# Column-strip sums of squares ahead of three FFNs, and shorter settling groups, in a two-block transformer kernel

## The reference

```
def rms(x, g):   return x * rsqrt(mean(x*x, -1) + 1e-6) * g
def ffn(x):      h = rms(x, norm); return (silu(h @ w_gate) * (h @ w_up)) @ w_down   # 1024 -> 2816 -> 1024

for l in (0, 1):                                  # first block
    x = x + 0.5 * ffn1(x)
    h = rms(x, mix_norm);  q, k, v, ... , gates = split(h @ w_in)
    x = x + merged(three attention branches, gates) @ w_out
    x = x + 0.5 * ffn2(x)
# second block: a state-space mixer with a context sequence, a Fourier mix, then one more FFN
```

## Time and profile before

| | before |
|---|---|
| median of 3 runs | 1607.89 us |
| profiled execution | 1608.59 us, of it 1606.8 us from the first to the last instruction |
| TensorE busy with matmuls | 1593.5 us (99%), 13104 records |
| VectorE, ScalarE, GpSimd busy | 1291.6, 927.2, 211.9 us |
| mean granted clock of TensorE | 0.999 of full speed |
| longest total wait of a TensorE line | 1.7 us |

### The profile page before, as it was taken

The page is one execution under the profiler, slowest core; times in us unless marked ns, Lnnn a source line. Parts: engine busy times, 40 slices in busy tenths (PEclk is TensorE's granted clock), DMA queues, the critical chain, the costliest instruction groups (busy, mean ns, idle before and its releaser), DMA issues.

```text
span 1606.8 us, 29855 instructions
## 1 busy us (share of the span) xinstructions
PE 1593.5 (99%) x13104; PEld 1530.3 (95%) x13104; DVE 1291.6 (80%) x1468; ACT 927.2 (58%) x1113; POOL 211.9 (13%) x125
## 2 busy tenths in 40 slices
PE   9999999999999999999999999999999999999998
PEld 8999988999999999999987899999999989899998
DVE  7887978688888987897878688785899788896655
ACT  7554655685465455554565677464546567754544
POOL 1000100000040001110010000032232378600000
PEclk9999999999999999999999999999999999999999
DMA  7677654444566665766754444555554345335552
GB/s 292 226 271 270 258 188 158 158 146 170 210 217 252 251 257 202 278 243 265 282 187 160 159 155 158 177 218 206 186 207 182 135 151 190 134 132 199 195 186 77
DMA packets 48408, 320.73 MB, mean 200 GB/s; under 512 B 5388, under 2 KB 8204, under 8 KB 10776
## 3 DMA queue, kind: packets, MB, share of 16 engines
q1 hardware_dynamic: 48136, 318.81, 54.0%
q10 hardware_dynamic: 144, 0.02, 0.0%
HBM read 317.74 MB, written 1.07 MB: 198 GB/s over the span
## 4 chain that ended last, share of the span: by engine, by line
PE 91%; DVE 5%; ACT 2%; DMA 1%; issue 0%; SPq 0%; DVEq 0%
PE ps L1240 26%; PE ps L1242 25%; PE ps L1241 25%; PE ps L1438 3%; PE ps L1440 3%; PE ps L1439 3%; DVE wlo L1913 1%; PE ps L1452 1%; ACT whi L692 1%; PE ps L1463 1%; DMA raw<-in_w_dram 1%; PE ps L1725 1%; DVE tmp L1913 1%; DVE qkA L1913 1%; DVE pre L2550 1%
## 5 line engine op out<-in xcount | busy, mean ns | idle before, releaser
L1913 DVE TENSOR_TENSOR wlo<-raw,whi 128x2048 fp32r<-128x2048 f32 (+2 forms) x255 | 583.7, 2297 | 94.3 <-ACT whi L692 90.6
L692 ACT ACTIVATE whi<-raw 128x2048 fp32r<-128x2048 f32 (+1 forms) x264 | 499.9, 1906 | 208.3 <-DMA raw<-in_w_dram 208.0
L1240 PE MATMUL ps<-h1hi,whi 128*128 128x256 f32 x1792 | 500.6, 279 | 1.5 <-DVE wlo L1913 1.5
L1241 PE MATMUL ps<-h1hi,wlo 128*128 128x256 f32 x1792 | 496.6, 277 | 0.0
L1242 PE MATMUL ps<-h1lo,whi 128*128 128x256 f32 x1792 | 496.6, 277 | 0.0
L1240 PEld LDWEIGHTS ps<-h1hi,whi 128*128 128x128 f32 x1792 | 337.8, 189 | 5.4 <-issue 2.3
L1241 PEld LDWEIGHTS ps<-h1hi,wlo 128*128 128x128 f32 x1792 | 337.7, 188 | 0.1
L1242 PEld LDWEIGHTS ps<-h1lo,whi 128*128 128x128 f32 x1792 | 337.4, 188 | 0.0
L1240 PE MATMUL ps<-hid_hi,whi 128*128 128x256 f32 x880 | 243.8, 277 | 0.0
L1242 PE MATMUL ps<-hid_lo,whi 128*128 128x256 f32 x880 | 243.1, 276 | 0.0
L1241 PE MATMUL ps<-hid_hi,wlo 128*128 128x256 f32 x880 | 243.1, 276 | 0.0
(11 more groups left out here) (376 smaller groups left out, 2592.6 us busy)
## 6 DMA issues: line engine op xcount, KB each, us to landing
raw<-in_w_dram SPq DMA_DIRECT2D x288, 1024.0 KB, 4.8
from_start<-decay_dram SPq DMA_DIRECT2D x3, 768.0 KB, 4.5
raw<-in_w_dram SPq DMA_DIRECT2D x8, 256.0 KB, 5.8
c_rows<-in_c_rows_dram SPq DMA_DIRECT2D x2, 1024.0 KB, 10.3
relbias<-in_relbias_dram SPq DMA_DIRECT2D x2, 1024.0 KB, 7.8
pv<-in_pv_dram SPq DMA_DIRECT2D x2, 641.0 KB, 7.6
xT<-in_x_dram SPq DMA_DIRECT2D x4, 256.0 KB, 5.0
raw<-in_w_dram SPq DMA_DIRECT2D x2, 512.0 KB, 6.9
```

Source lines behind the costliest of these rows:

```text
L692: act.activation(whi[:, slot, c], raw[:, slot, c], ACT.Copy).then_inc(hi_done[slot], 1)
L1240: pe.matmul(out, w_hi, hi, start=start, stop=False, skip_group_check=skip)
L1241: pe.matmul(out, w_lo, hi, start=False, stop=False, skip_group_check=skip)
L1913: return dve.tensor_tensor(out, a, b, op)
```

## The change

In `settle` the four matmuls read and write 16 columns each instead of 64. In `token_sums` the form without `token_major`, for every n but 0, becomes four matmuls on the four column strips, each with 128x32 ones and the same 128x256 moving tile; the last of them signals. Behind those sums (n = 2, 3, 5, the second to fourth FFN) `settle(6)` is no longer called. It stays in the first FFN, where the sum is inside the pieces, and in the fifth, which has its sums elsewhere.

```diff
         def settle(bank):
-            cols = ones[:, :].rearrange("p (m s n) -> p m s n", m=2, s=2)
             for q in range(4):
-                ins = pe.matmul(ps[32 * q:32 * q + 32, bank, 256:320].rearrange("p (m n) -> p m n", m=2), ones[:, 0:32],
-                                cols[:, :, q % 2, :], start=True, stop=True, tile_position=(0, 32 * q))
+                ins = pe.matmul(ps[32 * q:32 * q + 32, bank, 256:272], ones[:, 0:32], ones[:, 16 * q:16 * q + 16],
+                                start=True, stop=True, tile_position=(0, 32 * q))
             return ins
...
             pe.wait_ge(sq_added, n + 1)
-            ins = pe.matmul(ps[:, bank, 0:S], ones[:, :], sq[:, 0, :], start=True, stop=True)
+            if n > 0 and not token_major:
+                for q in range(4):
+                    ins = pe.matmul(ps[32 * q:32 * q + 32, bank, 0:S], ones[:, 0:32], sq[:, 0, :], start=True, stop=True,
+                                    tile_position=(0, 32 * q))
+            else:
+                ins = pe.matmul(ps[:, bank, 0:S], ones[:, :], sq[:, 0, :], start=True, stop=True)
...
             if 0 < n < NF3:
                 token_sums(n, False)
-            settle(6)
+            else:
+                settle(6)
```

## The result

| | before | after |
|---|---|---|
| median, same chip | 1608.34 us (22 runs, 1607.44 to 1611.84) | 1614.84 us (22 runs, 1607.72 to 1622.39) |
| profiled execution | 1608.59 us, span 1606.8 | 1616.24 us, span 1614.4 |

The ratio is 1.0031, some 5 us, with a 95% interval of 1.0021 to 1.0041; between the medians the kernel is slower by 6.5 us, where 1.3 us less was forecast, and outside the range. The new kernel also scatters: 9 of its 22 runs lie between 1607.7 and 1610.8, the other 13 above 1614.6. So most of the loss is something that happens in some executions and not in others, and one profile shows one of these outcomes.

A forecast was written before the change was run, and what follows sets the result against it. TensorE, with matmuls under way for 1593.5 of 1606.8 us, was taken as the bound. Settling groups 1.00 and sums 0.33 made 1.33 us off 1607.89: 1606.6 us, own range 1605.4 to 1607.8, 8 in 10 runs 1605.0 to 1609.3.

The forecast's parts named there:

- The costs of the edits: Savings forecast in TensorE's stream: 0.067 us for each of 15 groups, 0.11 us for each of three sums, 1.33 us together.
- Rival C: At the settling groups: fewer columns save nothing, only the sums' 0.33 us is gained, 1607.6 us; chance 0.12.
- Every return from work on column strips gives the quick speed, 22 of 22: TensorE's ordinary matmuls run at 113.3 ns, not 117.7, after column-strip work; 18 of the cases were settling groups.
- Rival A: 16-column groups no longer draw the quick speed: 1638.5 us if all fail (0.04), 1608 to 1613 at one or two places (0.05).
- the return at 1378: One of the 22 returns from column-strip work that the prediction counted as followed by the quick speed.
- It is drawn anew: TensorE's stream keeps its speed until plain fp32 work or a stall, then draws quick or slow, 4.4 ns a matmul apart.
- 0 +- 0.8 us: Term for some 2800 matmuls that no column strips precede: only a few stretches were expected to change speed.
- so it hides: VectorE's chain behind the sums loses 0.25 us against TensorE; 0.56 of 0.81 us stays at the fourth FFN's low hidden tile.
- at most 0.25 us a place: Cost bound where the later strip sum would make TensorE wait for VectorE, if the cover were gone.
- Rival B: Behind the three sums: strip sums don't settle, 768 matmuls run slow, 3.4 us, 1610.0 us; chance 0.06.

The follow-up runs named there:

- e6: Kernel before with 94 more settling groups in the FFNs (112 in all), all at 16 columns, a dense kernel: 1644.12 us, ratio 1.0222.
- e5: Kernel before with 94 more settling groups in the FFNs (112 in all), all at 64 columns, a dense kernel: 1649.67 us, ratio 1.0265.
- e1: Kernel before with only the three sums on column strips as in the new kernel, the other 15 groups at 64 columns: 1608.25 us, ratio 0.9998.
- e10: Kernel before with every settling group made of eight matmuls of 16 columns, each strip used twice: 1609.36 us, ratio 1.0003.
- e7: New kernel, but the third FFN has the old wide sum with a 16-column group behind it: 1610.06 us, ratio 1.0009.
- e8: New kernel with one group widened to 64 columns, ahead of i = 3 in the third FFN: 1611.51 us, ratio 1.0018.
- e12: New kernel with two groups at 64 columns, ahead of i = 3 in the third FFN and ahead of the fifth FFN: 1615.48 us, ratio 1.0039.
- e15: New kernel with 64 columns at four groups (first FFN's, third FFN's i = 3, two of the fourth FFN), eleven at 16: 1607.74 us, ratio 0.9995.
- e16: New kernel with 64 columns only at the first FFN's group behind its first two chunks: 1608.30 us, ratio 1.0008.
- e17: New kernel with all fifteen settling groups at 48 columns instead of 16: 1607.98 us, ratio 0.9991.

## Why the prediction was wrong

- **The costs of the edits** held: 0.064 for 0.067 us a group, 0.34 for 0.33 us in the sums, 1.30 for 1.33 in all. Rival C (no saving from fewer columns) is refuted, by the traces and by e6 against e5.
- **"Every return from work on column strips gives the quick speed, 22 of 22" is the step that failed.** It was a count of cases that all had 64 columns or more, and it was applied to 16. Two of its returns that weren't settling groups were luck of one trace: `strips`, slow in 14 of 17 profiles, and the return at 1378, slow in 5 of 17. What the runs put in its place: a group of 48 or 64 columns that stands alone makes the stream quick whatever came before (211 of 211), one of 16 entered directly from the slow stream leaves it slow in 11 of 15 and from the quick one quick in 129 of 129. Rival A named this mechanism, but as "fails" or "doesn't" with 0.09 in all. It asked at how many places the group fails, and the answer hangs on what is ahead of each. The trace of before showed that in part: the first FFN's group was entered from a slow stream, and two stood behind 24-column matmuls and transposes. The two of the third FFN were entered from the quick stream there; the stall put them at risk.
- **"It is drawn anew" at each piece of plain fp32 work** doesn't hold either. Behind the two transposes the stream has the other speed than ahead of them, 14 of 14, and the term "0 +- 0.8 us" for such stretches came out as 267 fewer slow matmuls, 1.2 us.
- **The second step that failed: "so it hides".** The delay of the later sum was compared with the distance in the fourth FFN alone (0.81 us before; after, the hidden tile is written by 1082.36 and read from 1083.05, 0.69 left, where 0.56 was forecast). The shorter distance was that of the low weights in the third FFN, written by 651.12 and first needed by the load at 651.38, and it wasn't looked up. The prediction priced such a miss at "at most 0.25 us a place"; the stall of 0.07 us is within that, but it cost 6.0 us in the profile of after, since the stream went on slow behind it where nothing wide enough followed.
- **Rival B** (strip sums don't settle) is refuted, 25 of 25 and e1.
- **The median**: the forecast took one profile's speeds for the kernel's. The first FFN (6.6 us) and the third (6.0 us) go either way from profile to profile, while the 384 of the fourth were slow in all seven profiles with a 16-column group ahead of them (dense kernels apart, e10's counted), and the 192 behind them then quick: 0.85 us net. The 168 behind these were slow in three of the seven (0.74 us). How often an execution comes out slow differs from kernel to kernel even where the code of the first FFN is the same: e7, e8 and e12 have 1 of 11, 6 of 12 and 5 of 5 runs over 1612.5, for a reason that no run shows. So what share of the loss belongs to which FFN is open, as is why the stream has two speeds at one clock and why 48 columns reset it where 32 don't. An idea of the expectations, that a pass must outlast the load of a strip's weights (estimated at 26 ns, against 27 for a pass of 32 columns and 40 for 48), is only argued, and it doesn't explain the pairs of e5.

## What to carry to other kernels

Before a "dummy" operation is made cheaper, find out what state it restores and from which state it is entered; count the cases by the state ahead of them, not all together. On an engine that never waits, list every producer that the edit delays, since a stall of 0.07 us was followed here by 6.0 us of loss. And where runs scatter more after a change than before, one profile shows one outcome: look at the list of times first.

## What the runs showed of the hardware

- The stream of fp32r matmuls (128x128 weights, 256 columns) has two stable spacings at the granted clock 1.00, 113.3 and 117.8 ns. Each was held over 622 steps (e1 and the new kernel, behind i = 7 of the third FFN). A stall of 0.07 us can turn the quick one into the slow one, and need not: the stall in the third FFN was followed by the slow stream in the new kernel and e12, by the quick one in e1, e8, e15, e16 and e17.
- A group of four fp32 matmuls on column strips, standing alone, was followed by the quick one in 211 of 211 cases with 48 or 64 columns, in 15 of 18 with 32 and in 181 of 203 with 16. Two such groups of 64 in a row left the other speed than they found in 5 of 5 (e5), `strips` in 17 of 17.
- A VectorE subtraction with two SBUF operands beside GpSimd's took 7.70 us (e16) and 7.84 us (e5) instead of 2.29, and ended behind the last of four GpSimd instructions that ran on end to end. The Trainium skill (SBUF — State Buffer, SBUF: two separate sides) says that the engine that starts first holds the shared ports for its whole instruction and the other blocks. The durations agree (4.42 for 2.4 on GpSimd's side in e15); that the one that waits can lose several turns in a row is shown only by e16 and e5.
